# Loading the memory rows by column pieces for both row tiles, and folding their norm weight into rounding and rest

## The reference, cut to what matters

```python
def rms_norm(x, g):
    y = xf * lax.rsqrt(jnp.mean(xf * xf, axis=-1, keepdims=True) + NORM_EPS)
    return (y * g.astype(jnp.float32)).astype(x.dtype)

kv_m = rms_norm(mem, mem_norm_g[l]) @ w_mem_kv[l]     # mem: 256 x 1024, w_mem_kv: 1024 x 1024
k_m, v_m = jnp.split(kv_m, 2, axis=-1)                # groups KM and VM of the kernel
h = rms_norm(x, norm_g[l]); proj = h @ w_in[l]        # the groups after them: FH, QH, ...
```

## Time and profile before

| | |
|---|---|
| median of 3 runs | 1340.68 us (1340.37 to 1341.74) |
| the profiled execution, its own time | 1340.78 us |
| its span, first to last instruction | 1339.0 us |
| mean granted TensorE clock | 0.999 |
| TensorE busy | 1323.3 us (99%), 7049 matmuls |
| VectorE busy | 934.2 us (70%) |
| ScalarE busy | 740.5 us (55%) |

### The profile page before, as it was taken

How to read it: one execution, slowest core, us unless ns; L and a number is a source line. 1 busy time by engine, 2 the same in 40 slices (tenths; PEclk the granted TensorE clock), 3 DMA queues, 4 the chain that set the end, 5 groups by cost and what they waited for, 6 DMA issues and landing times.

```text
span 1339.0 us, 17869 instructions
## 1 busy us (share of the span) xinstructions
PE 1323.3 (99%) x7049; PEld 1132.6 (85%) x7049; DVE 934.2 (70%) x1238; ACT 740.5 (55%) x1057; POOL 97.5 (7%) x126
## 2 busy tenths in 40 slices
PE   9999999999999999999999999999999999999998
PEld 7988888978888899888878888889988887888886
DVE  6789876699876497786885555466696778655544
ACT  6864775675684466444465444456754445544432
POOL 1002000001200001500000000000123000000000
PEclk9999999999999999999999999999999999999999
DMA  8654335455236355644464565635564445466552
GB/s 285 219 179 154 98 126 183 164 172 174 95 126 222 107 196 181 191 157 142 157 221 127 188 189 173 232 134 185 185 188 157 157 142 189 156 189 188 189 182 101
DMA packets 140291, 227.67 MB, mean 170 GB/s; under 512 B 8400, under 2 KB 55312, under 8 KB 139952
## 3 DMA queue, kind: packets, MB, share of 16 engines
q1 hardware_dynamic: 137968, 221.67, 50.5%
q0 software_dynamic: 576, 2.23, 1.0%
q10 hardware_dynamic: 1664, 2.63, 0.5%
HBM read 225.33 MB, written 1.18 MB: 169 GB/s over the span
## 4 chain that ended last, share of the span: by engine, by line
PE 91%; DVE 5%; ACT 2%; issue 1%; POOL 1%; DMA 1%; SPq 0%; ACTq 0%; DVEq 0%
PE gp L694 70%; PE gp L682 9%; PE mp L662 4%; DVE arena L1591 2%; PE mp L1007 2%; DVE wt_rest L1597 1%; PE mp L823 1%; PE mp L890 1%; POOL rs_out L2411 1%; PE mp L865 1%; PE mp L844 1%; PE mp L851 1%; ACT first_hi L1194 1%; DMA wt<-in_w_mem_kv 1%; DVE small L2147 0%
## 5 line engine op out<-in xcount | busy, mean ns | idle before, releaser
L1597 DVE TENSOR_TENSOR wt_rest<-wt,wt_hi 128x1024 fp32r<-128x1024 f32 x148 | 174.5, 1221 | 80.8 <-ACT wt_hi L1194 78.8
L1194 ACT ACTIVATE mix_hi<-wt 128x1024 fp32r<-128x1024 f32 x128 | 132.5, 1059 | 129.3 <-PE gp L694 99.2
L1194 ACT ACTIVATE wt_hi<-wt 128x1024 fp32r<-128x1024 f32 x148 | 148.0, 1053 | 95.3 <-DMA wt<-in_ffn_down 48.6
L1597 DVE TENSOR_TENSOR wt_rest<-wt,mix_hi 128x1024 fp32r<-128x1024 f32 x128 | 151.9, 1230 | 46.7 <-ACT mix_hi L1194 46.0
L1597 DVE TENSOR_TENSOR wt_rest<-wt,first_hi 128x1024 fp32r<-128x1024 f32 x104 | 124.0, 1221 | 26.0 <-ACT first_hi L1194 25.1
L2411 POOL TENSOR_TENSOR rs_out<-rs_in,minus_half 128x1 f32<-128x1 f32 (+3 forms) x35 | 54.0, 1544 | 1178.0 <-DVE rs_in L1602 1178.0
L694 PE MATMUL gp<-mix_hi,mix_hT_hi 128*128 128x512 f32 x320 | 127.0, 397 | 0.9 <-DVE wt_rest L1597 0.9
L694 PE MATMUL gp<-wt_hi,hT_hi 128*128 128x512 f32 x320 | 126.8, 396 | 0.0
L1194 ACT ACTIVATE first_hi<-wt 128x1024 fp32r<-128x1024 f32 x104 | 105.7, 1059 | 36.9 <-PE gp L694 26.1
L694 PE MATMUL gp<-wt_hi,hT_rest 128*128 128x512 f32 x320 | 125.0, 391 | 0.0
L694 PE MATMUL gp<-wt_rest,mix_hT_hi 128*128 128x512 f32 x320 | 124.8, 390 | 0.0
(11 more groups left out here) (347 smaller groups left out, 2991.4 us busy)
## 6 DMA issues: line engine op xcount, KB each, us to landing
wt<-in_w_in SPq DMA_DIRECT2D x96, 1024.0 KB, 5.1
wt<-in_w_out SPq DMA_DIRECT2D x20, 1024.0 KB, 5.1
wt<-in_ffn_gate SPq DMA_DIRECT2D x40, 512.0 KB, 4.0
wt<-in_ffn_up SPq DMA_DIRECT2D x40, 512.0 KB, 5.0
wt<-in_ffn_down SPq DMA_DIRECT2D x20, 1024.0 KB, 5.1
wt<-in_w_mem_kv SPq DMA_DIRECT2D x7, 1024.0 KB, 5.2
arena<-in_w_in SPq DMA_DIRECT2D x4, 1024.0 KB, 8.2
wt<-in_w_branch_pool SPq DMA_DIRECT2D x4, 1024.0 KB, 5.0
```

Source lines behind the costliest of these rows:

```text
L1194: nc.scalar.activation(rounded_part(u)[:, k:k + nk, :], raw_of(u)[:, k:k + nk, :], ACT.Copy)\
L1597: return nc.vector.tensor_tensor(o, i0, i1, ALU.subtract)
```

## The change

The memory rows come in three pieces of columns, each for both row tiles: columns 0 to 255, 256 to 511 and 512 to 1023. SP sends them in turn with the two parts of unit 0. Step `memT{i}` now transposes the two blocks of columns 2i and 2i+1 of both tiles, which is just what part i needs. The gained copy in SBUF (`mem_s`) is no longer made for layer 0: ScalarE rounds straight from the bank with the norm weight as its scale (two instructions of 128x256 a step), and VectorE makes the rest from the bank with one fused multiply and subtract (two of 128x256 a step). TensorE makes each pair of column blocks in its turn: transposes of the next pair between the parts of KM. ScalarE's squares of the memory and its mem_hat copies both stand after all rounding of the memory and of parts 0 to 3, and each mem_hat copy waits for the rest of its pair.

```diff
+MEM_PIECES = ((0, 2 * P), (2 * P, 4 * P), (4 * P, D))
...
+        def memory_columns(i):
+            return bank(f"memT{i}", 4, P).rearrange("p (t k) i -> p t k i", t=TT)
...
-            for t in range(TT):
-                sp.dma_start(region(a_S, TT, D)[:, t], w["mem"][0, t * P:(t + 1) * P, :]).then_inc(loaded[f"mem{t}"], 16)
             (dst, src), = unit_loads(0)
-            for k, signal in ((0, first_part), (PART_K, w_loaded[0])):
-                sp.dma_start(dst[:, k:k + PART_K], src[:, k:k + PART_K]).then_inc(signal, 16)
+            mem_rows = w["mem"][0].rearrange("(t p) d -> p t d", p=P)
+            for i, (c0, c1) in enumerate(MEM_PIECES):
+                sp.dma_start(region(a_S, TT, D)[:, :, c0:c1], mem_rows[:, :, c0:c1]).then_inc(loaded[f"mem{i}"], 16)
+                if i < 2:
+                    k = PART_K * i
+                    sp.dma_start(dst[:, k:k + PART_K], src[:, k:k + PART_K]).then_inc((first_part, w_loaded[0])[i], 16)
...
-            for i in range(4):
-                t, q = divmod(i, 2)
-                transposes(f"memT{i}", [region(a_S, TT, D)[:, t, (4 * q + j) * P:(4 * q + j + 1) * P] for j in range(4)],
-                           (loaded[f"mem{t}"], 16))
-
+            def memory_transposes(i):
+                transposes(f"memT{i}", [region(a_S, TT, D)[:, t, k * P:(k + 1) * P] for t in range(TT) for k in (2 * i, 2 * i + 1)],
+                           (loaded[f"mem{min(i, 2)}"], 16))
+            memory_transposes(0)
             idle_products(4)
...
             def first_unit_parts():
-                state["unit"] += 1
+                state["unit"] += 2
                 pe.wait_ge(sig("mem_rounded"), 1)
-                split_part(0, (0,), terms=(0,))
+                split_part(0, range(TT), terms=(0,))
+                memory_transposes(1)
                 pe.wait_ge(sig("mem_scaled"), 1)
-                split_part(0, (0,), terms=(1, 2))
-                pe.wait_ge(sig("mem_scaled"), 2)
-                split_part(0, (1,)).then_inc(w_used, 1)
-                split_part(1, range(TT)).then_inc(w_used, 1)
+                split_part(0, range(TT), terms=(1, 2)).then_inc(w_used, 1)
+                for n in range(1, 4):
+                    if n < 3:
+                        memory_transposes(n + 1)
+                    pe.wait_ge(sig("mem_scaled"), n + 1)
+                    split_part(n, range(TT)).then_inc(w_used, 1)
...
-            def round_memory(t, q):
-                act.wait_ge(sig("mem_gained"), 2 * t + q + 1)
-                nc.scalar.activation(mem_hi[:, t, 4 * q:4 * q + 4, :], mem_s[:, t, 4 * q:4 * q + 4, :], ACT.Copy).then_inc(sig("mem_rounded"), 1)
+            def round_memory(i):
+                act.wait_ge(*computed(f"memT{i}"))
+                for k in range(2):
+                    ins = nc.scalar.activation(mem_hi[:, :, 2 * i + k, :], memory_columns(i)[:, :, k, :], ACT.Copy, scale=col("mem_norm_g", 0)[:, 2 * i + k:2 * i + k + 1])
+                ins.then_inc(sig("mem_rounded"), 1)
...
-            square_memory(0)
-            round_memory(0, 0)
-            round_weights(1)
-            round_memory(1, 0)
-            round_weights(2)
-            round_memory(0, 1)
-            square_memory(1)
-            round_weights(3)
-            round_memory(1, 1)
-            round_weights(4)
+            round_memory(0)
+            round_weights(2)
+            round_memory(1)
+            round_memory(2)
+            round_weights(4)
+            round_memory(3)
+            for i in range(len(MEM_PIECES)):
+                act.wait_ge(loaded[f"mem{i}"], 16)
+            square_memory(0)
+            square_memory(1)
             for i in range(4):
-                t, q = divmod(i, 2)
-                nc.scalar.activation(mem_hat[:, t, 4 * q:4 * q + 4, :], bank(f"memT{i}", 4, P), ACT.Copy)\
-                    .then_inc(step_read[STEP_NO[f"memT{i}"] % 4], 1)
+                act.wait_ge(sig("mem_scaled"), i + 1)
+                nc.scalar.activation(mem_hat[:, :, 2 * i:2 * i + 2, :], memory_columns(i), ACT.Copy).then_inc(step_read[STEP_NO[f"memT{i}"] % 4], 1)
...
-            gain_memory(0, 0)
-            gain_memory(0, 1)
-            rest_of_memory(0, 0)
-            gain_memory(1, 0)
-            weight_rests(1)
-            rest_of_memory(1, 0)
+            rest_of_memory(0)
             weight_rests(2)
-            gain_memory(1, 1)
-            rest_of_memory(0, 1)
-            weight_rests(3)
-            rest_of_memory(1, 1)
+            rest_of_memory(1)
+            rest_of_memory(2)
             weight_rests(4)
+            rest_of_memory(3)
             dve.wait_ge(sig("mem_squared"), TT)
```

More of the change, by code:

```diff
@@ L422, in mixer_program @@
         mp = ctx.enter_context(nc.psum_tensor("mp", [P, 4, F32_COLS], F))
-        loaded = {n: sem("loaded_" + n) for n in ("ident", "const", "const2", "gain0", "rows", "rows_b", "x", "mem0", "mem1", "gain1", "early", "late", "ba", "flips", "lower", "masks")}
+        loaded = {n: sem("loaded_" + n) for n in ("ident", "const", "const2", "gain0", "rows", "rows_b", "x", "mem0", "mem1", "mem2", "gain1", "early", "late", "ba", "flips", "lower", "masks")}
         w_loaded = [sem(f"w_loaded{i}") for i in range(SLOTS)]
@@ L619, in _ @@
                     elif l == 0:
-                        sp.wait_ge(sig("mem_gained"), 4 + TT)
+                        sp.wait_ge(sig("mem_gained"), TT)
                         sp.wait_ge(sig("hg_factors"), 9 * DEPTH)
@@ L806, in _ @@
                     first_unit_parts()
-                    split_units(s("KM"), 1, tile_ready=lambda t: (sig("mem_scaled"), TT + t + 1))
                     columns()
@@ L1204, in _ @@
             act.dma_start(small[0:16, 0:P], w["mem_norm_g"].rearrange("l (k p) -> (l k) p", p=P)).then_inc(loaded["gain0"], 16)
-            def round_memory(t, q):
-                act.wait_ge(sig("mem_gained"), 2 * t + q + 1)
-                nc.scalar.activation(mem_hi[:, t, 4 * q:4 * q + 4, :], mem_s[:, t, 4 * q:4 * q + 4, :], ACT.Copy).then_inc(sig("mem_rounded"), 1)
+            def round_memory(i):
[3 more added lines that the diff above has]
+                ins.then_inc(sig("mem_rounded"), 1)
             def square_memory(t):
-                act.wait_ge(loaded[f"mem{t}"], 16)
                 nc.scalar.activation(region(R1["Z0"], TT, D)[:, t], region(a_S, TT, D)[:, t], ACT.Square, accum_out=small[:, 364 + t:365 + t])\
                     .then_inc(sig("mem_squared"), 1)
-            square_memory(0)
-            round_memory(0, 0)
-            round_weights(1)
-            round_memory(1, 0)
-            round_weights(2)
-            round_memory(0, 1)
+            act.wait_ge(*read_out("colM"))
+            round_memory(0)
[6 more added lines that the diff above has]
+                act.wait_ge(loaded[f"mem{i}"], 16)
+            square_memory(0)
             square_memory(1)
-            round_weights(3)
-            round_memory(1, 1)
-            round_weights(4)
             for i in range(4):
-                t, q = divmod(i, 2)
-                nc.scalar.activation(mem_hat[:, t, 4 * q:4 * q + 4, :], bank(f"memT{i}", 4, P), ACT.Copy)\
-                    .then_inc(step_read[STEP_NO[f"memT{i}"] % 4], 1)
+                act.wait_ge(sig("mem_scaled"), i + 1)
+                nc.scalar.activation(mem_hat[:, :, 2 * i:2 * i + 2, :], memory_columns(i), ACT.Copy).then_inc(step_read[STEP_NO[f"memT{i}"] % 4], 1)
             for l in range(DEPTH):
@@ L1367, in _ @@
                     for t in range(TT):
-                        act.wait_ge(sig("mem_gained"), 4 + t + 1)
+                        act.wait_ge(sig("mem_gained"), t + 1)
                         nc.scalar.activation(mem_hi[:, t], mem_s[:, t], ACT.Copy).then_inc(sig("mem_rounded"), 1)
@@ L1645, in _, with rest_of_memory @@
             evac(copy(cols[:, 0:16], bank("colM", 16)), "colM")
[L1646 to L1654, removed]
-            gain_memory(0, 0)
-            gain_memory(0, 1)
-            rest_of_memory(0, 0)
-            gain_memory(1, 0)
-            weight_rests(1)
-            rest_of_memory(1, 0)
+            def rest_of_memory(i):
+                dve.wait_ge(sig("mem_rounded"), i + 1)
+                for k in range(2):
+                    ins = nc.vector.scalar_tensor_tensor(mem_rest[:, :, 2 * i + k, :], memory_columns(i)[:, :, k, :],
+                                                         col("mem_norm_g", 0)[:, 2 * i + k:2 * i + k + 1], mem_hi[:, :, 2 * i + k, :].bitcast(F),
+                                                         ALU.mult, ALU.subtract)
+                ins.then_inc(sig("mem_scaled"), 1)
+            rest_of_memory(0)
             weight_rests(2)
-            gain_memory(1, 1)
-            rest_of_memory(0, 1)
-            weight_rests(3)
-            rest_of_memory(1, 1)
+            rest_of_memory(1)
+            rest_of_memory(2)
             weight_rests(4)
+            rest_of_memory(3)
             dve.wait_ge(sig("mem_squared"), TT)
```

## The result

The changed kernel takes 1346.93 us (median of 6 runs, 1346.32 to 1348.72), the kernel before 1340.64 beside it. The ratio is 1.0050, 95% interval 1.0040 to 1.0060: 6.3 us slower, where +2.9 was forecast and the range ended at 1346.6. The profiled execution took 1346.63 us, with a span of 1344.8 for 1339.0. The mean granted clock was 0.995 to 0.997 in all six executions; in the profile of the kernel before it is 0.999.

A forecast was written before the change was run, and what follows sets the result against it. TensorE, busy 1323.3 of 1339.0 us, was taken as the bound. VM starting 2.9 us later, with KM's 1.1 us gain lost in the wait, gave 1340.78 + 2.9 = 1343.7 us; range 1341.6 to 1346.6.

The forecast's parts named there:

- ScalarE's queue behind pair 3: ScalarE after rounding pair 3: two memory squares and four mem_hat copies delay x, so VM starts 2.9 us later.
- The steps behind the square of x: From x's first square at 20.3 through VectorE's norming and column copies to VM's products at 26.7 us.
- Landings: DMA queue at the start: pieces placed by bytes on the old landing curve, unit 1 landing at 13.1 us.
- First products: Start of KM: first products from 8.0 us, some 2 us of started work earlier; later landings then set the pace.
- ScalarE rounds pair 0 from 6.15 to 6.97: ScalarE's first rounding of the memory, 0.82 us long, followed by part 0 until 8.0 us.
- The first square of x: On ScalarE behind the mem_hat copies: starts at 20.3 us for 17.27, +3.0 us.
- KM ends 1.1 us sooner: TensorE's end of KM: 20.95 us for 22.03, the gain going into the wait before VM.
- TensorE's clock: TensorE between KM and VM, 20.95 to 26.7 us: whether the faster pace holds through two 2 us waits; sum left at 1343.7.
- rival 1: Clock falls between KM and VM, slowing xT2, xT3 and VM's first products: +1.5 to +3 us, 1345.2 to 1346.7; 18%.
- Slower: Whole kernel: measured above 1343.4 us, about 0.2% from no change; chance 58%.
- the hole: TensorE between KM and VM: idle about 2 us before xT0 and about 2 us again before xT2.

The follow-up runs named there:

- b1: The kernel before with only its two squares of the memory moved behind the rounding of parts 0 to 3: 1342.77 us, ratio 1.0013.
- c3: c1 with the two squares of the memory moved earlier on ScalarE and 2 fill products for 7 in the first hole: 1343.42 us, ratio 1.0021.
- c2: Changed kernel, table early, memory squares moved, 6 idle products for 4, squares of x before mem_hat copies, colA and colB copies before part 4's rest: 1340.60 us.
- c1: Changed kernel with an early tiny ScalarE copy, 6 idle products for 4 behind memT0, and 7 in each of two later TensorE waits: 1344.60 us, ratio 1.0028.
- a1: Changed kernel with one tiny ScalarE copy ahead of the first rounding, so the activation table loads at the start: 1345.96 us, ratio 1.0036.
- d4: c2 run once more, unchanged, on the chip of three other follow-up kernels: 1341.07 us, ratio 1.0001 to the kernel before.
- a4_old_loads: Changed kernel with the old loads (memory tile 0, tile 1, then unit 0's two parts), every memory transpose waiting for both tiles: 1349.66 us, ratio 1.0067.
- a2_fill: Changed kernel with 8 more idle products on TensorE before xT0 and 8 between xT1 and xT2: 1346.59 us, ratio 1.0044.
- a3_squares: Changed kernel with its squares of the memory moved on ScalarE, one behind pair 1's rounding, one ahead of pair 3's: 1344.53 us, ratio 1.0028.

## Why the prediction was wrong

**The main mechanism was right.** "ScalarE's queue behind pair 3 is the part that sets the end" was shown by b1 (+1.9 us in the kernel before from it alone) and by c3 (-1.2 from moving two squares); c2, which undoes the whole loss with the orders, the early table and two idle products together, agrees. The steps behind the square of x came out as written: its start to VM's, 6.4 forecast (26.7 - 20.3), 6.5 in c1 with the clock up (27.04 - 20.52). Landings were well placed too: 0a came at 5.8, 0b at 9.2, piece 2 at 10.6 and unit 1 at 13.2, for 5.5, 9.0, 10.4 and 13.1. Piece 0 came at 1.17 + 2.7 = 3.9, ahead of the 4.69 at which TensorE took it, which is sooner than the 4.91 that the prediction read as the end of the idle products: before, the memory's own landing stood there. Its issue (size, us to landing):

```profile
arena<-in_mem SPq DMA_DIRECT2D x1, 256.0 KB, 2.7
```

**Step "First products", mis-sized: "ScalarE rounds pair 0 from 6.15 to 6.97".** It began at 7.12, since the table's load of 1.28 us stands behind the wait for memT0. I took the load for hidden at the start, as before, and didn't ask which instruction would be the first of ScalarE and how many waits it has. The first product came at 9.05 for 8.0 and pair 3's rounding at 16.20 for 15.57. The first square of x was +3.65 for +3.0; with the table early it started 0.46 (a1) and 0.40 (c1) sooner, so the table is 0.4 to 0.5 of this 0.65. "KM ends 1.1 us sooner" came out as 0.14. Set against the landing of unit 1 the pieces can be read apart from the luck of the landings: KM ends about 9.0 us behind it in the four profiles of the kernel before and its variants (12.9 to 21.87), 8.0 in all six with the early table (13.0 to 20.99 in d4), 8.5 in the changed kernel (13.2 to 21.73). So the late table took 0.5 of the 1.0 us that the pieces give, and unit 1 landed 0.3 later in this profile.

**The step that failed: "TensorE's clock".** I let the sum stay at 1343.7 by the row of a 1.06 us wait and gave the fall 18%. It fell: the last eight transposes at 0.21 us each cost 0.8 us and seven products of VM 1.4, 2.2 us where the sum had nothing. That is within the "+1.5 to +3" of rival 1; a third place, the wait before the first product, was not in it at all. Over the runs, c1 against a1 puts the clock at 1.0 to 1.4 us once the table is early; against the changed kernel c1 is 2.3 us lower (2.2 with each beside its own before), of which the earlier square of x (20.92 to 20.52) is 0.4, which leaves 1.8 to 1.9. The sum of the measured terms is 3.65 + 0.8 + 1.4 = 5.85 us of span, for 5.8 seen. That it fits this well is luck: the time from VM's start to the end differs between the profiles by up to 1 us with the clock up (1315.0 to 1316.0). Rival 1's own range was 1345.2 to 1346.7; with the 0.65 of the later square of x on top, the measured 1346.9 lies inside.

**The chances.** "Slower" at 58% was right in sign. The error in judgement was to treat rivals as alternatives where one is the consequence of the other: the clock falls in, or behind, waits such as the forecast itself predicted. All six executions of the changed kernel have a mean clock of 0.995 to 0.997; all seven of c1, with these waits filled, have 0.998 or 0.999. The waits make the fall likely and not certain, since a1 kept them and has one execution at 0.999.

**What the change brought.** KM's end is sooner by 0.1 us as it stands; with the repairs 0.9 to 1.4 (20.49 in c2 and 20.99 in d4 for 21.87), of which 0.5 in c2 is its early landing. At VM's start 0.5 to 1.0 of it is left, since the order on VectorE takes 0.36 back; in the medians nothing can be measured. An order with the squares of x first and the rest of part 4 still ahead of the copies of the columns was not run.

## What to carry to other kernels

When work is moved to the end of an engine's queue because "it isn't urgent", ask what stands behind it there: here two squares and four copies, whose results were not needed before the end of KM, held up the rows of the next stage by some 3 us. If a forecast contains a new wait of TensorE, price the clock with it; idle products on zeros in the waits are a cheap test, and here they gave 1.0 to 1.4 us. Look at what ScalarE's first activation waits for: here the table's load stood behind one of its two waits, and a tiny activation with one early wait ahead of it took it out.

## What the runs showed of the hardware

The clock fell in places that differ between the profiles: in the changed kernel and a4_old_loads in the hole (0.50 from 28.2 to 31.3 and from 28 to 34), in a2_fill around part 0's products (0.52 from 8.5 to 12), in a3_squares behind them (0.50 from 11 to 14), in the others nowhere. The wait ahead of each fall was 1.87, 1.89, 2.38 and 1.80 us; behind waits of 1.06 (before), 1.60 (the changed kernel ahead of 9.05, b1) and 1.64 us (a1) the faster level held. No limit follows from that, since other executions of a1 with the same waits have a lower mean clock. The Trainium skill, "TensorE: Matmul & The Clock Gate", "HAM oscillation — how this bites in real kernels", tells of this from waits for DMA of 3 to 5 us; the waits here were shorter, and it happened all the same. The profile's clock column doesn't show the first microseconds: it has 1.00 at 5.8 to 7.2, while the sixteen transposes there took 3.13 us for 1.81.

The table's load took 1.28 us and ScalarE's first rounding followed 0.01 us behind it (5.83 + 1.28 to 7.12). It ran at 1.19 us in the profiles whose first activation has one wait (before, b1, a1) and behind memT0, at 5.64 to 7.47, in those where it has two (the changed kernel, a2, a3, a4). The Trainium skill, "ScalarE: Activation LUTs", "What ACT_TABLE_LOAD costs", gives 1283 ns for it, which agrees, and for a switch to another set a drain of 1380 ns besides. This trace doesn't show it at the first load, nor at the later one of 57.25 us, whose next activation starts at 58.54.
